# Residual projections with the weight's high half used once: one 512-column product into two halves of a bank, added by VectorE

## The reference, cut to what matters

```python
    # first_block, layer 0 and layer 1
        x = x + mix.astype(x.dtype)      # mix ends with  y @ out_w   (mamba2)  or  o @ out_w  (attention)
        ff = conv_ffn(x, ...)            # ends with  (silu(gate) * up) @ down_w
        x = x + ff.astype(x.dtype)
    # second_block
        h = h + ga1 * jnp.dot(merged, w_out[l])
        ...
        h = h + ga2 * jnp.dot(jax.nn.silu(gte) * val, w_down[l])
    return rms_norm_2(h, g_final)
```

## Time and profile before

| | |
|---|---|
| median of three runs | 1181.27 us (1180.33 to 1183.52) |
| span of the profiled execution, first to last instruction | 1179.3 us |
| time outside the span, by the median less the span | 2.0 us |
| PE busy | 1149.0 us (97%), 9336 products and as many loads |
| DVE busy | 920.6 us (78%) |
| ACT busy | 699.8 us (59%) |
| POOL busy | 184.7 us (16%) |
| chain that ended last | PE 78%, DVE 13%, ACT 4%, issue 2%, transfers 2% |
| mean granted clock of PE | 0.989 of 2.4 GHz |

### The profile page before, as it was taken

One profiled execution on the slowest core, in us unless ns is written; L12 is line 12 of the kernel. 1 busy time (PEld: TensorE's weight loads), 2 busy tenths in 40 slices (PEclk: granted clock), 3 DMA queues, 4 the chain that ended last, 5 costly groups with the idle time before them and its releaser, 6 DMA issues.

```text
span 1179.3 us, 24322 instructions
## 1 busy us (share of the span) xinstructions
PE 1149.0 (97%) x9336; PEld 1118.0 (95%) x9336; DVE 920.6 (78%) x1591; ACT 699.8 (59%) x1011; POOL 184.7 (16%) x233
## 2 busy tenths in 40 slices
PE   7999999999999999999999999899999999999998
PEld 6999989999999999999999999899988998999997
DVE  5988776788888878777888877569997778888653
ACT  6767774466665457875766643554875346566631
POOL 0000231111112200001111121101332101333200
PEclk9999999999999999999999999999999999999999
DMA  7465446655556864334555578475335744555540
GB/s 265 177 208 181 144 139 222 251 183 187 185 182 243 312 225 147 141 108 161 180 178 181 175 271 283 150 254 193 117 130 173 258 165 173 179 181 183 177 172 36
DMA packets 43714, 220.23 MB, mean 187 GB/s; under 512 B 8063, under 2 KB 12656, under 8 KB 22640
## 3 DMA queue, kind: packets, MB, share of 16 engines
q1 hardware_dynamic: 31552, 185.25, 44.7%
q0 software_dynamic: 9264, 30.94, 7.4%
q10 hardware_dynamic: 2816, 2.90, 0.8%
HBM read 217.97 MB, written 1.11 MB: 186 GB/s over the span
## 4 chain that ended last, share of the span: by engine, by line
PE 78%; DVE 13%; ACT 4%; issue 2%; DMA 2%; POOL 0%; DVEq 0%; ACTq 0%
PE ps L848 70%; DVE wl L548 4%; ACT wh L541 2%; DMA ada_w<-in_w_ada 2%; DVE work L2167 1%; PE ps L997 1%; DVE work L2324 1%; DVE ada_w L2132 1%; PE ps_idle L1073 1%; PE ps L1114 1%; DVE work L2145 1%; DVE small L2695 1%; PE ps L1117 1%; DVE xl L2162 0%; PE ps L975 0%
## 5 line engine op out<-in xcount | busy, mean ns | idle before, releaser
L848 PE MATMUL ps<-xh,wl 128*128 128x256 f32 x1776 | 512.4, 288 | 7.7 <-DVE wl L548 5.2
L848 PE MATMUL ps<-xl,wh 128*128 128x256 f32 x1776 | 506.4, 285 | 0.0
L848 PE MATMUL ps<-xh,wh 128*128 128x256 f32 x1776 | 505.9, 285 | 0.0
L548 DVE TENSOR_TENSOR wl<-raw,wh 128x2048 fp32r<-128x2048 f32 (+1 forms) x178 | 401.3, 2256 | 79.2 <-ACT wh L541 78.8
L541 ACT ACTIVATE wh<-raw 128x2048 fp32r<-128x2048 f32 (+1 forms) x178 | 333.2, 1874 | 100.5 <-PE ps L848 93.6
L848 PEld LDWEIGHTS ps<-xh,wl 128*128 128x128 f32 x1776 | 344.6, 194 | 15.9 <-issue 7.8
L848 PEld LDWEIGHTS ps<-xl,wh 128*128 128x128 f32 x1776 | 344.9, 194 | 0.3 <-issue 0.2
L848 PEld LDWEIGHTS ps<-xh,wh 128*128 128x128 f32 x1776 | 344.7, 194 | 0.0
L848 PE MATMUL ps<-actr,wh 128*128 128x256 f32 x1888 | 340.6, 283 | 0.0
L848 PEld LDWEIGHTS ps<-actr,wh 128*128 128x128 f32 x1888 | 294.4, 192 | 0.0
L848 PE MATMUL ps<-actr,wl 128*128 128x256 f32 x944 | 268.6, 285 | 4.5 <-DVE actr L3039 2.5
(11 more groups left out here) (269 smaller groups left out, 1081.1 us busy)
## 6 DMA issues: line engine op xcount, KB each, us to landing
raw<-in_up SPq DMA_DIRECT2D x66, 1024.0 KB, 4.9
ada_w<-in_w_ada POOLq DMA_DIRECT2D x62, 256.0 KB, 5.0
raw<-in_xbc SPq DMA_DIRECT2D x12, 1024.0 KB, 5.1
work<-in_w_ada POOLq DMA_DIRECT2D x34, 256.0 KB, 6.0
raw<-in_z SPq DMA_DIRECT2D x8, 1024.0 KB, 4.9
raw<-in_so SPq DMA_DIRECT2D x8, 1024.0 KB, 5.1
raw<-in_dn0a SPq DMA_DIRECT2D x8, 1024.0 KB, 6.4
raw<-in_dn1a SPq DMA_DIRECT2D x8, 1024.0 KB, 5.6
```

What stands on the lines that cost most here:

```text
L548: nc.vector.tensor_tensor(wl[:, b % RING, 0:n], raw[:, b % RING, 0:n], wh[:, b % RING, 0:n].bitcast(F32), ALU.subtract).then_inc(lo_done, 1)
L848: mm = nc.tensor.matmul(o, l, r, start=start and n == 0, stop=stop and n == 2)
```

## The change

The high and the low half of each operand are now neighbours in one buffer (`whl`, `xhl`, and `hhl`, `yhl`, `ohl`, `mhl` in `actr`), with the same sizes in all. In the six residual projections a k-step is now two products (`mm3_halves`): the high weight by the high and the low activation in one product of 512 columns, which fills both halves of the bank, and the low weight by the high activation, 256 columns, into the first half. DVE adds both halves to `x` (`add_halves`), the second half first, then a wait on its own semaphore, then the first. In each projection the last tile (m = 7) keeps three products of 256 columns and one add. All other stages keep `mm3`.

```diff
+HALVES = ("dn0", "dn1", "dn2", "ao0", "ao1", "ao2", "ao3", "wout")
...
-        wh = sb("wh", [P, RING, SLOT], F32R)
-        wl = sb("wl", [P, RING, SLOT], F32R)
+        whl = sb("whl", [P, RING, 2, SLOT], F32R)
+        wh, wl = whl[:, :, 0, :], whl[:, :, 1, :]
...
-        xh = sb("xh", [P, KD, T], F32R)
-        xl = sb("xl", [P, KD, T], F32R)
+        xhl = sb("xhl", [P, KD, 2, T], F32R)
+        xh, xl = xhl[:, :, 0, :], xhl[:, :, 1, :]
...
+            def mm3(o, w, xs, start, stop):
+
+                nc.tensor.matmul(o, w[:, 1], xs[:, 0], start=start, stop=False)
+                nc.tensor.matmul(o, w[:, 0], xs[:, 1], start=False, stop=False)
+                return nc.tensor.matmul(o, w[:, 0], xs[:, 0], start=False, stop=stop)
+
+            def mm3_halves(o, w, xs, start, stop):
+
+                nc.tensor.matmul(o, w[:, 0], xs.rearrange("p c b -> p (c b)"), start=start, stop=False)
+                return nc.tensor.matmul(o[:, 0:T], w[:, 1], xs[:, 0], start=False, stop=stop)
...
+                            if name in HALVES and not (i * RING // 3 == 3 and t == 1 and kind == PAIR3
+                                                       or kind == TWO and j + RING * i == 3 and t == 1):
+                                mm = mm3_halves(bank(g), whl[:, r, :, off:off + P], X[:, k], st, en)
+                            else:
+                                mm = mm3(bank(g)[:, 0:T], whl[:, r, :, off:off + P], X[:, k], st, en)
...
+                    if s < 7:
+                        mm = mm3_halves(bank(g), whl[:, b % RING, :, o:o + P], yhl[:, k], k == 0, k == 15)
+                    else:
+                        mm = mm3(bank(g)[:, 0:T], whl[:, b % RING, :, o:o + P], yhl[:, k], k == 0, k == 15)
...
+            def add_halves(m, g, scale):
+
+                def part(cols):
+                    src = bank(g)[:, cols]
+                    if scale is None:
+                        return V.tensor_tensor(x[:, m, :], src, x[:, m, :], ALU.add)
+                    return V.scalar_tensor_tensor(x[:, m, :], src, scale(m), x[:, m, :], ALU.mult, ALU.add)
+
+                if m < KD - 1:
+                    step.add(part(slice(T, 2 * T)))
+                    step.wait()
+                give_back(part(slice(0, T)), g)
```

More of the change, by code:

```diff
@@ L438, in W, with halves_of @@
             return a
-        def R(off, a, b):
-            return actr[:, off:off + a * b].rearrange("p (a b) -> p a b", b=b)
+        def halves_of(off, n):
+            both = actr[:, off:off + 2 * n * T].rearrange("p (a c b) -> p a c b", c=2, b=T)
+            return both, both[:, :, 0, :], both[:, :, 1, :]
         KB = 256
@@ L842, in _, with mm3_by_token @@
         def _(pe):
[L843 to L849, removed]
+            def mm3(o, w, xs, start, stop):
[5 more added lines that the diff above has]
+                return nc.tensor.matmul(o[:, 0:T], w[:, 1], xs[:, 0], start=False, stop=stop)
+            def mm3_by_token(o, xs, w, start, stop):
+                nc.tensor.matmul(o, xs[:, 0], w[:, 1], start=start, stop=False)
+                nc.tensor.matmul(o, xs[:, 1], w[:, 0], start=False, stop=False)
+                return nc.tensor.matmul(o, xs[:, 0], w[:, 0], start=False, stop=stop)
             def two_slabs(slabs, ready):
@@ L947, in slab_tile @@
                     off = k * 256 + t * P
-                    mm = mm3(bank(g)[:, 0:T], (wh[:, b % RING, off:off + P], wl[:, b % RING, off:off + P]),
-                             (X[0][:, k, :], X[1][:, k, :]), k == 0, k == KD - 1, False)
+                    if name in HALVES and (name, t) != ("ao3", 1):
+                        mm = mm3_halves(bank(g), whl[:, b % RING, :, off:off + P], X[:, k], k == 0, k == KD - 1)
+                    else:
+                        mm = mm3(bank(g)[:, 0:T], whl[:, b % RING, :, off:off + P], X[:, k], k == 0, k == KD - 1)
                 if ks[-1] == KD - 1:
@@ L1214, in ffn @@
                 if norm in DEFERRED:
-                    stream(f"up{f}", (xh, xl), x_ready(use), deferred=(norm, r))
+                    stream(f"up{f}", xhl, x_ready(use), deferred=(norm, r))
                 else:
                     norm_sum(norm, r)
-                    stream(f"up{f}", (xh, xl), x_ready(use))
-                stream(f"dn{f}", (hh, hl), lambda k: pe.wait_ge(low_done, LOW0 + NF * f + k + 1))
+                    stream(f"up{f}", xhl, x_ready(use))
+                stream(f"dn{f}", hhl, lambda k: pe.wait_ge(low_done, LOW0 + NF * f + k + 1))
             ffn(0, "n1", 1, 1)
@@ L1309, in _ @@
             scores(1)
[L1310 to L1311 removed]
+            slab_tile("q1", 0, x2hl)
+            slab_tile("q1", 1, x2hl)
             token_tile("v0", 0)
@@ L1446, in _ @@
             for s in range(4):
-                stream(f"yr{s}", (xh, xl))
+                stream(f"yr{s}", xhl)
             for s in range(4):
-                stream(f"xr{s}", (xh, xl))
+                stream(f"xr{s}", xhl)
                 if 0 < s < 3:
@@ L1464, in _ @@
                     gates(h + 2)
-            stream("woa", (ah, al), lambda k: pe.wait_ge(al_done, k + 1))
+            stream("woa", ahl, lambda k: pe.wait_ge(al_done, k + 1))
             pe.wait_ge(rl_done, 8)
-            stream("wor", (rh, rl))
-            stream("wout", (mh, ml), lambda k: pe.wait_ge(ml_done, k + 1))
+            stream("wor", rhl)
+            stream("wout", mhl, lambda k: pe.wait_ge(ml_done, k + 1))
             ffn(2, "n5", 6, 5)
@@ L2213, in residual @@
                         wait_tile(dve, name, s // RING, s % RING, t, cnt)
-                        if scale is None:
-                            ins = V.tensor_tensor(x[:, m, :], bank(g)[:, 0:T], x[:, m, :], ALU.add)
-                        else:
-                            ins = V.scalar_tensor_tensor(x[:, m, :], bank(g)[:, 0:T], scale(m), x[:, m, :],
-                                                         ALU.mult, ALU.add)
-                        give_back(ins, g)
+                        add_halves(m, g, scale)
                         if to:
```

72 lines of the change are left out of this document (31 added, 41 removed).

## The result

The changed kernel takes 1186.75 us (median of 7 runs, 1184.47 to 1190.82) against 1181.27 (median of 7, 1177.89 to 1184.82): the ratio is 1.0055, 95% interval 1.0035 to 1.0074. It is slower by half a per cent. The profiled execution has a span of 1184.4 us at a mean granted clock of 0.986; before it was 1179.3 at 0.989. So I forecast the wrong sign, and the range of 1170 to 1183 doesn't hold the time.

What follows compares the result with a forecast made beforehand. PE's pace was taken to bound dn0, dn1 and dn2, DVE with ACT the later part of ao and wout. Stage terms 0.95 + 2.3 - 1.2 + 3.1 - 3.5 + 3.7 = 5.4 us off 1181.3; predicted 1176.0, range 1170 to 1183.

Steps and rivals of the forecast that it cites:

- What a k-step gains: Residual projections' k-steps: wide product 0.216 us, other 0.120, so 0.336 against 0.360, a gain of 24 ns.
- so: In so, DVE's extra adds set the pace after an earlier start; gain 0.95 of the 2.7 us PE saved.
- dn0: In dn0, 116 k-steps up to the last slab gain 2.8 us, the end loses 0.45; net gain 2.3.
- ao: In ao, extra adds of tiles 2 to 6 lengthen the chain PE waits on; net 1.2 us slower.
- dn1: In dn1, 148 k-steps before the last slab gain 3.55 us, the end loses 0.45; net gain 3.1.
- wout: In wout, second adds delay the norm product while PE's saving is hidden; net 3.5 us slower, the worst stage.
- dn2: In dn2, all 154 k-steps gain, 3.7 us; tile 6's second add fits in DVE's 1.34 us wait.
- rival (a): All residual projections: columns set the pace, PE gains nothing and the adds stay; 1187.7 us, chance 0.12.
- Rival (b): Residual projections: each product carries its own 13 ns, so a k-step gains 13, not 24; 1181 us, chance 0.13.
- Rival (d): Longer PE waits in ao and wout cost clock, 1.5 us of slower products behind each; 1179 us, chance 0.13.

Runs made afterwards that it cites:

- pace: The changed kernel plus 156 extra products of several widths in the idle bank, put in at a busy and a quiet place; 1231.82 us in one run.
- busy: The changed kernel with products nobody reads filling TensorE's waits at the ends of ao and wout; 1181.13 us, 1.0012 to the kernel before.
- adds: Second additions kept, but k-steps of three separate 256-column products except each tile's first; 1188.43 us, 1.0056 to the kernel before.
- ao_wout: The change made in ao and wout only, other stages as in the kernel before; 1192.37 us, 1.0098 to the kernel before.

## Why the prediction was wrong

The step that failed is the one under "What a k-step gains": "I take 0.216 for it, 3 ns more than its columns, and 0.120 for the other product: 0.336 against 0.360, a gain of 24 ns". Measured: 0.236 and 0.117, together 0.353, a gain of 6.6 ns. I had two rows of longer products without the extra 13 ns. The half-clock row didn't bear on the full clock: `pace` shows that 13 ns come on top of 256, 384 and 512 columns alike at the full clock, and the half clock has none even for 256. And from products of one column at 0.106 I took it that the load was the pace of a 256-column product. The 128-column products (112 ns) do sit at such a floor; 256 columns lie above it, at columns plus 13. L1098's plain float32 isn't the same kind of product: the rows of `keep_busy`, plain float32 too, start 0.215 to 0.217 us apart at the full clock in `busy`, two passes of 256 columns and some 2 ns, where 512 columns of the split type take 0.227. The alternation of 512 and 256 then took 6 ns of the 13 that were left, for a reason that stays open.

Point by point, in us of gain, as predicted, as the two profiled executions have it, and what the same working gives with 6.6 ns:

- `so`: 0.95; 0.42 by the norm product (227.23 against 227.65 in the earlier trace rows); about 0.35. Its sign came: tile 7's addition starts at 225.24 without a wait, and PE waits for its low half (226.78).
- `dn0`: 2.3; 0.37 by the norm product; 116 x 0.0066 - 0.45 = 0.3.
- `ao`: -1.2; the norm product in `up1` came 2.1 later than it came in, and another 1.6 by half clock: -3.7; about -1.7. My sign for it was a wait of over 3 us before k-step 6. It was 2.38 between starts, and the rest stood ahead of `up1`, in the wait for tile 4's bank, which my working didn't have.
- `dn1`: 3.1; 0.53 by the norm product (746.17 against 743.85, 2.85 late coming in); 0.98 - 0.45 = 0.5.
- `wout`: -3.5; -3.3 at the norm product, and 20.0 from the first low half was 20.06. This step held, and so did its reason, that PE's saving is hidden: `adds` gave the same rows without the saving. Behind the norm another 0.9 went by half clock.
- `dn2`: 3.7; 1.02; 154 x 0.0066 = 1.0. That tile 6's second addition fits in the wait held: `adds` lost nothing in `dn2`.

With that one term corrected my own sums give 0.35 + 0.3 - 1.7 + 0.5 - 3.55 + 1.0 = -3.1. The profiled executions have -5.1; the other 2.0 are for the most part 1.6 and 0.9 of half clock behind `ao` and `wout`, less 0.4 that came back where other dips fell differently. My rival (a) had the right side, its place (`ao` and `wout`) and its point of decision (a gain under 13 ns), and its 1187.7 is 1 us off; its reason, that the columns alone set the pace, is wrong. That its number is so near is in part luck: it has neither what PE gained in the four other stages, 2.3 us by the list above, nor the 2.5 us of half clock, and these cancel. Rival (b) had the right law for one product and the wrong sum for two kinds in turn. Rival (d) is borne out in part, and I shouldn't have set it against the others: half clock followed the waits behind `ao` and `wout`, more of it than before, and filling them brought 5 us back. I had priced it at 3 us. That it came because the waits had grown isn't shown. The same 1.59 us were followed by a clock of 0.76, 0.88 and 1.00 in three kernels; and over its runs `adds`, with the same second additions, has a mean clock of 0.990, near the 0.991 of the kernel before, while the changed kernel has 0.986 and `ao_wout` 0.985. The dip in `wout` itself (1.1 us by PE's slabs) cost nothing, since DVE sets the time there.

By ratios the layout is 0, the wide products -5.2, the second additions +6.6; the sum would be +1.4 and the whole is +6.5. The 5 us between may be what the wide products save where nobody can use it (`ao`, `wout`) and the clock, but these runs don't show it: every ratio is uncertain by 2 us or more, and a sum of three by some 4.

## What to carry over

Before fusing products to save a product's fixed cost, get that cost at the clock at which it will be paid: a few dozen idle products of each width in a bank that nobody reads cost one run and give it to the nanosecond. Put them in the order of the real stream too, since 512 and 256 in turn cost 6 ns more than their sum. Put work on an engine only in the stages in which it waits: the same edit was worth 3.2 us of PE's time in four stages and cost 11.6 us (7.6 to 15.6) in the other two. And look for half clock behind every wait of TensorE. It differs from run to run, so judge it by the mean clock of many runs; where a wait can't be shortened, try filling it with products that nobody reads.

## What the runs showed of the hardware

- In full-clock series of one width, a product of this type with its own load takes 112 ns for 128 columns (a floor), 120 for 256, 173.5 for 384 and 227 for 512 (`pace`): from 256 up, columns at 2.4 GHz and 13 ns. At half clock it takes its columns at 1.2 GHz and nothing more, 213 for 256 and 0.43 us for 512 (957.51 to 957.94 above). The Trainium skill, "TensorE: Matmul & The Clock Gate", section "Back-to-back issue gap", has N / 2.4 + 2.5 ns for an isolated warm product: in these streams of loads and products the trace agrees with the form from 256 columns up, and has 13.3 in the place of 2.5.
- At the start of a series it takes up to seven products until the pace is steady (for 512: 233, 236, 228, 233, 231, then 227; for 384 six or seven), and in steady alternation of 512 and 256 the pattern repeats every three pairs. These figures are the same within 2 ns with a DMA share of 0.60 and VectorE busy for 7.0 of 13 us as with a share of 0.00 and 1.4 of 24 us. 256 and 384 in turn (293), or 128 and 512 (340), cost no more than their sum.
- For 256 columns the extra is 7 ns instead of 13 with a weight of 64 columns, but 9 with 96 and 11 with 32. A series of 512 columns gains nothing from the smaller weight: 230 with 64 and 231 with 32.
- The time of a run goes with its mean granted clock: over the 29 runs of the kernel before in one comparison, 1175.4 to 1185.7 us, the correlation is -0.7, and 0.001 of clock goes with 0.8 us. So about half of the spread between runs goes with how much half clock a run has. The waits for `ada_w` ahead of `wout`, 2.0 to 6.2 us from one profiled execution to another, are a second source.
